# Nearest 128 keys and values moved as one 12288 B packet a partition instead of two of 6144 B

## The chip, the cores and the metric

One NeuronCore of a Trainium2 chip runs the whole kernel. The metric is the device time of one execution in microseconds. The kernel before took 404.59 us, the median of three runs (402.63, 404.59 and 405.35).

## The reference

Two decoder layers run over two groups of tokens that share the weights: a prompt of 256 tokens from position 0, and 8 sample sequences with one new token each at position 2048. Everything is float32, with a model width of 1024. Each layer normalises x, multiplies it by one input projection whose columns are split among three groups, and adds the output projection of their results to x:

```
A: a_val * sigmoid(a_glu) -> causal depthwise conv of width 31 -> LayerNorm -> silu, times silu(gate)   384 channels
B: trailing means over 2/4/8/16 positions minus the token -> 64x64 maps -> scale, times silu(gate)      256 channels
C: 6 heads of 64; keys at offsets d*j, j = 0..128, for d = 1, 4, 16; the three patterns merged by
   their softmax denominators, times silu(gate)                                                       384 channels
x = x + W_out[concat(A, B, C)]
```

For the samples the keys and values of the last 2048 positions come in as caches, one row of 384 floats (1536 B) for each sequence, position and layer. The outputs contain these caches too, moved on by one position, with the new row at the end: 8 sequences x 2047 rows x 1536 B, for keys and values and for both layers. The pattern with d = 1 needs the nearest 128 rows, the one with d = 4 every fourth row of the nearest 512, the one with d = 16 every sixteenth row of all 2048.

## The kernel before

**Who does what.** TensorE runs the projections (`pj`, 33 column tiles of 128 from `PROJ`, then 8 of the output projection, each of 8 matmuls over 264 tokens), attention and transposes. VectorE runs the 93 convolution taps of a layer (L1296), the sample scores (`tok`, `ssc`) and the products with the gates. ScalarE does the activations. The order of the steps on each engine is written out in `SCHEDULE`, `DVE_SCHEDULE` and `ACT_SCHEDULE`.

**Three DMA queues.** The queue of SP (q1 in the profile) gathers the rows that the samples attend to into `kg` and `vg` (L479, function `gather`) and stores keys back from `kg` (L459, L463, L465, function `store_rows`). The queue of ACT (q10) loads the weight tiles `wt`, 4096 B a partition and up to 14 tiles ahead (L874), and stores values back from `vg`, in the steps of the output projection (`STORES`). The queue of POOL (q0) copies the rest of the caches from HBM to HBM (L600), in packets of at most 7680 B. All three run beside each other from the start.

**The gathers.** `GATHER` cuts the 2048 rows of a sequence into three spans. The nearest one is rows 1920 to 2047, all of them: 16 partitions take 8 neighbouring rows each, which lie together in HBM and in SBUF, 8 x 1536 = 12288 B. The middle span takes every fourth row, 6 a partition, and the far span every sixteenth, 6 a partition; each of their rows is a run of 1536 B by itself. The argument `max_dma_last_dim=NEAR_BYTES` limits the run that one packet moves; with 6144 B it cuts only the runs of the nearest span, into two. There are 8 sequences, two kinds (k and v) and two layers, so 32 gathers of the nearest span, and 32 stores of it: 64 transfers of 16 partitions.

**Order on SP.** Early loads, then for layer 0 the nearest rows of `kg` (8 transfers), a table, the other spans of `kg`, all of `vg`, small loads, the stores of keys (16), a wait at L543 until these have landed, the gather of `kg` for layer 1 and so on. At the end SP stores y (L549 to L557) and then waits for every copy and store (L559 to L567).

**Waits on the gathers.** VectorE waits at L1230 for all three spans of `kg` before the first sample product (step `("sprod", 0)`, L1234). TensorE waits at L761 for `vg`. ScalarE waits at L879 for `vg` before it issues the stores of values.

Of the kernel before, what the change touches and what calls it, by code (L numbers as in the profile page):

```python
# [27 lines left out]
C_CONV, C_POOL, C_ATT, HD = 384, 256, 384, 64  # L28
# [17 lines left out]
GATHER = []  # L46
# [178 lines left out]
BLOCK_BYTES = (FAR_STEP - 1) * C_ATT * 4  # L225


NEAR_BYTES = 4 * C_ATT * 4
IN_FLIGHT = 16
assert DEPTH * NCOPIES % IN_FLIGHT == 0  # L230

# [17 lines left out]
def sample_rows(s):  # L249

    first = 2 * PER_S * (s // 2) + s % 2
    return slice(first, first + 2 * PER_S - 1, 2)
# [56 lines left out]
def trunk_program(nc, ins, const, const_at, angles, outs):  # L309
    (y_prompt, y_sample, o_conv_p, o_pool_p, o_k_p, o_v_p, o_conv_s, o_pool_s, o_k_s, o_v_s) = outs  # L310
    with ExitStack() as ctx:
# [140 lines left out]
        def store_rows(eng, kind, l, s):  # L452
# [3 lines left out]
            for (lo, d, n), name in zip(GATHER[:2], ("near", "far")):  # L456
                rows = out[:, s, lo - 1:lo - 1 + d * n * PER_S].rearrange("o (a b e) h d -> (o a) b e (h d)", a=PER_S, e=d)
                at = SLOT_OF[d]
                eng.dma_start(rows[:, :, 0, :], frm[part, at:at + n, :], max_dma_last_dim=NEAR_BYTES).then_inc(S[f"{kind}_{name}_out"], 16)  # L459
            if (kind, l) in DEEP:  # L460
# [7 lines left out]
        def _(sp):  # L468
# [3 lines left out]
            def gather(kind, l, to, name, spans=GATHER):  # L472

                for lo, d, n in spans:
                    at = SLOT_OF[d]
                    for s in SAMPLE_ORDER:
                        rows = one(f"cache_{kind}_win", l)[:, s, lo:lo + d * n * PER_S]
                        rows = rows.rearrange("o (a b e) h d -> (o a) b e (h d)", a=PER_S, e=d)[:, :, 0, :]
                        sp.dma_start(to[sample_rows(s), at:at + n, :], rows, max_dma_last_dim=NEAR_BYTES).then_inc(S[name], 16)  # L479

# [924 lines left out]
```

## Time and profile before

| | |
|---|---|
| median of the runs | 404.59 us |
| the profiled execution | 401.57 us |
| its span | 399.7 us |
| TensorE busy | 347.5 us (87%) |
| VectorE busy | 232.6 us (58%) |
| DMA | 44329 packets, 157.73 MB, mean 395 GB/s |

The span is what the profiler saw between the first and the last event; 1.9 us of the execution lie around it. DMA packets are counted one for each contiguous run that a DMA engine moves, and one for each small write to a semaphore at the end of a transfer. The core has 16 DMA engines, and a share of 100% means that all 16 moved packets all the time; since the records of neighbouring packets overlap a little, a saturated stretch shows slightly over 1.

### The profile page before, as it was taken

What the parts mean: (1) busy time and instruction counts of PE and PEld (TensorE: products, weight loads), DVE (VectorE), ACT (ScalarE), POOL (GpSimd) and SP (SyncE); (2) the same over time, 40 slices, a digit from 0 to 9 for tenths busy, and PEclk for the clock granted to TensorE, in tenths of its full rate; (3) what the DMA queues carried; (4) which work ended last, traced back from release to release, by engine and by line L of the source; (5) the groups of instructions that cost most, each with busy time, mean ns of one, the idle gap of its engine ahead of it and who ended that gap; (6) DMA issues with size and microseconds to landing.
All of it is one profiled execution on the core that took longest, in us unless ns stands there. A gap on an engine that the chain in (4) does not pass through costs nothing.

```text
span 399.7 us, 4745 instructions
## 1 busy us (share of the span) xinstructions
PE 347.5 (87%) x1550; PEld 273.4 (68%) x1550; DVE 232.6 (58%) x530; ACT 100.2 (25%) x237; POOL 58.8 (15%) x110
## 2 busy tenths in 40 slices
PE   3898799999889859899948999999979877989990
PEld 2686578887667636588827888888757654758870
DVE  2604669859977976620103489978984997541010
ACT  4200012542523123500111011453352222320011
POOL 4006830000600002044000420000600011000000
PEclk9999969999889899999986999999979988989997
DMA  8999999999999999999999999999999999999983
GB/s 293 412 419 412 418 418 417 418 407 411 417 419 408 418 392 406 396 418 418 416 398 387 414 418 416 417 411 420 418 419 417 414 357 361 372 374 372 396 347 118
DMA packets 44329, 157.73 MB, mean 395 GB/s; under 512 B 6988, under 2 KB 20116, under 8 KB 44306
## 3 DMA queue, kind: packets, MB, share of 16 engines
q0 software_dynamic: 14624, 88.25, 54.6%
q10 hardware_dynamic: 14420, 41.52, 26.3%
q1 hardware_dynamic: 15262, 27.67, 18.7%
q8 instruction: 12, 0.20, 0.2%
q14 instruction: 11, 0.09, 0.1%
HBM read 140.23 MB, written 104.46 MB: 612 GB/s over the span
## 4 chain that ended last, share of the span: by engine, by line
PE 43%; DVE 13%; SPq 12%; ACTq 11%; DMA 10%; issue 5%; ACT 4%; DVEq 0%
PE pj L693 23%; SPq L479 11%; DMA kg<-in_cache_k_win 10%; PE pj L836 8%; ACTq L459 4%; DVE yc L1296 3%; ACTq L465 3%; PE psc L765 3%; PE ptr L611 3%; DVE ssc L1240 2%; ACTq L463 2%; PE ps L813 1%; ACTq L874 1%; DVE spsum_pad L1266 1%; DVE tok L1234 1%
## 5 line engine op out<-in xcount | busy, mean ns | idle before, releaser
L693 PE MATMUL pj<-hT,wt 128*128 128x264 f32 x800 | 197.9, 407 | 6.3 <-DVE hT L1151 4.5
L693 PEld LDWEIGHTS pj<-hT,wt 128*128 128x128 f32 x800 | 159.0, 202 | 39.7 <-issue 11.6
L1296 DVE SCALAR_TENSOR_TENSOR yc<-u_ext,par,yc 128x256 f32<-128x256 f32 x180 | 77.2, 481 | 3.8 <-DVE u_smp L1180 1.0
L836 PE MATMUL pj<-mix,wt 128*128 128x264 f32 x256 | 61.2, 395 | 0.0
L836 PEld LDWEIGHTS pj<-mix,wt 128*128 128x128 f32 x256 | 49.1, 194 | 8.5
L600 POOL DMA_DIRECT2D out<-in_cache_v_win x48 | 26.2, 554 | 142.3 <-issue 142.3
L1366 DVE TENSOR_TENSOR xT<-xT,pj 128x264 f32<-128x264 f32 x16 | 6.9, 430 | 55.9 <-PE pj L836 55.9
L600 POOL DMA_DIRECT2D out<-in_cache_k_win x48 | 26.5, 561 | 83.6 <-issue 83.6
L954 ACT ACTIVATE ex<-pj 128x264 f32<-128x264 f32 x22 | 8.6, 391 | 78.3 <-PE pj L693 45.2
L1178 DVE SCALAR_TENSOR_TENSOR u_ext<-ex,pj 128x256 f32<-128x256 f32 x6 | 2.5, 422 | 30.5 <-ACT ex L954 30.5
L1234 DVE TENSOR_TENSOR tok<-kg,qb 128x1536 f32<-128x1536 f32 x10 | 17.6, 1758 | 3.4 <-DMA kg<-in_cache_k_win 3.0
L1240 DVE TENSOR_REDUCE ssc<-tok 128x24 f32<-128x1536 f32 x10 | 17.5, 1753 | 0.8 <-DVE mix L1187 0.3
L908 ACT ACT_TABLE_LOAD x12 | 15.4, 1283 | 6.7 <-issue 4.7
L765 PE MATMUL psc<-vg,spm_pad 128*64 128x384 f32 x80 | 14.9, 510 | 0.0
L1187 DVE SCALAR_TENSOR_TENSOR mix<-ex,pj 128x264 f32<-128x264 f32 x16 | 6.9, 429 | 13.3 <-ACT ex L954 12.9
L611 PE MATMUL ptr<-cst,sc 128*128 128x128 f32 x36 | 6.3, 285 | 7.0 <-DVE sc L1213 6.9
L1020 ACT ACTIVATE sc<-sc,nmax 128x128 f32<-128x128 f32 x12 | 4.8, 402 | 28.4 <-DVE nmax L1206 25.1
L1075 ACT ACTIVATE hT<-xT 128x264 f32<-128x264 f32 x8 | 3.4, 423 | 33.2 <-DVE xT L1366 26.7
L611 PEld LDWEIGHTS ptr<-cst,sc 128*128 128x128 f32 x36 | 4.0, 141 | 10.9 <-DVE sc L1213 10.5
L813 PE MATMUL ps<-yc,ones 128*128 128x264 f32 x12 | 5.2, 599 | 6.7 <-DVE yc L1296 6.7
L937 ACT ACTIVATE sqg<-pj 128x264 f32<-128x264 f32 x12 | 4.7, 391 | 24.7 <-PE pj L693 22.7
L1202 DVE SCALAR_TENSOR_TENSOR sc<-psc,cst 128x384 f32<-128x384 f32 x12 | 6.6, 553 | 6.6 <-PE psc L732 6.6
(187 smaller groups left out, 339.6 us busy)
## 6 DMA issues: line engine op xcount, KB each, us to landing
wt<-in_w_tiles ACTq DMA_DIRECT2D x62, 512.0 KB, 33.2
out<-in_cache_k_win POOLq DMA_DIRECT2D x24, 1080.0 KB, 44.4
out<-in_cache_v_win POOLq DMA_DIRECT2D x24, 1080.0 KB, 81.1
out<-in_cache_k_win POOLq DMA_DIRECT2D x8, 1200.0 KB, 72.7
out<-in_cache_v_win POOLq DMA_DIRECT2D x8, 1200.0 KB, 87.9
out<-in_cache_k_win POOLq DMA_DIRECT2D x16, 432.0 KB, 65.1
out<-in_cache_v_win POOLq DMA_DIRECT2D x16, 432.0 KB, 86.2
kg<-in_cache_k_win SPq DMA_DIRECT2D x32, 144.0 KB, 36.0
```

Source lines behind the costliest of these rows:

```text
L459: eng.dma_start(rows[:, :, 0, :], frm[part, at:at + n, :], max_dma_last_dim=NEAR_BYTES).then_inc(S[f"{kind}_{name}_out"], 16)
L465: eng.dma_start(rows[:, 0, :], frm[part.start + 2:part.stop:2, DEEP_AT, :]).then_inc(S[f"{kind}_deep_out"], 16)
L479: sp.dma_start(to[sample_rows(s), at:at + n, :], rows, max_dma_last_dim=NEAR_BYTES).then_inc(S[name], 16)
L600: pool.dma_start(dst, src, max_dma_last_dim=size).then_inc(copy_out[n % IN_FLIGHT], 16)
L611: return nc.tensor.transpose(out, in_, C["ident"][0:rows, 0:rows])
L693: last = nc.tensor.matmul(pj[n % RING][:, 0:T], wt[:, g % WRING, k, :], hT[:, k, :], start=(k == 0), stop=(k == KD - 1))
L765: nc.tensor.matmul(psc[o:o + SV_HALF, 0:C_ATT], spm_pad[:, j * NH * NS:j * NH * NS + SV_HALF], v, start=(j < 2), stop=(j >= SLOTS - 1))
L836: last = nc.tensor.matmul(pj[n % RING][:, 0:T], wt[:, g % WRING, k, :], mix[:, k, :], start=(k == 0), stop=(k == KD - 1))
L908: nc.scalar.preload_act_table_set(TABLE_BEFORE[step])
L1234: V.tensor_tensor(tok[:, :, :], kg[:, a:b, :], qb[:, None, :].to_broadcast([P, b - a, C_ATT]), ALU.mult).then_inc(S["kprod_ok"], 1)
L1240: last = V.tensor_reduce(ssc[:, a:b, :], tok[:, :, :].rearrange("p j (h d) -> p j h d", h=NH), AX.X, ALU.add)
L1296: last = V.scalar_tensor_tensor(out=yc[:, t, 0:SEQ], in0=x_w, scalar=par[:, ROW_CW + w * CT + t:ROW_CW + w * CT + t + 1], in1=yc[:, t, 0:S ...
```

## The change

`NEAR_BYTES` becomes `GATHER[0][2] * C_ATT * 4` = 8 x 384 x 4 = 12288, in place of 4 x 384 x 4 = 6144. It is used at L459 (stores of the nearest and the middle span) and L479 (gathers of all spans).

```
-NEAR_BYTES = 4 * C_ATT * 4
+NEAR_BYTES = GATHER[0][2] * C_ATT * 4
```

## Rows read from the trace of the kernel before

**Rows 1.** The page: span, engines' busy time, DMA share in 40 slices, packets
```profile
span 399.7 us, 4745 instructions
PE 347.5 (87%) x1550; PEld 273.4 (68%) x1550; DVE 232.6 (58%) x530; ACT 100.2 (25%) x237; POOL 58.8 (15%) x110
DMA  8999999999999999999999999999999999999983
DMA packets 44329, 157.73 MB, mean 395 GB/s; under 512 B 6988, under 2 KB 20116, under 8 KB 44306
```

**Rows 2.** The page's DMA queues: packets, MB, share of 16 engines over the span
```profile
q0 software_dynamic: 14624, 88.25, 54.6%
q10 hardware_dynamic: 14420, 41.52, 26.3%
q1 hardware_dynamic: 15262, 27.67, 18.7%
```

**Rows 3.** Stages: stage, length, busy time by engine, clock, DMA share, GB/s
```profile
50.00:88.00 38.00, 37.70 (x164) 31.73 (x165) 28.09 (x70) 13.37 (x33) 3.76 (x7) 0.92 1.02 414
380.00:392.00 12.00, 9.45 (x47) 7.36 (x45) 1.98 (x4) 2.22 (x5) 0.00 (x0) 1.00 0.81 314
392.00:399.70 7.70, 0.00 (x0) 0.00 (x0) 0.00 (x0) 0.00 (x0) 0.00 (x0) 0.63 0.28 101
```

**Rows 4.** Waits of SP's queue from 390 to 400 us: total, times, longest
```profile
SPq L563 <- DMA out<-vg: 5.7, 2, 4.8
SPq L561 <- DMA out<-in_cache_v_win: 0.7, 1, 0.7
```

**Rows 5.** Timeline, the last DMA that SP issues: start, duration
```profile
391.57 0.35 SPq L557 DMA_DIRECT2D out<-qk  x1
```

**Rows 6.** DMA queues from 394 to 399.7 us: packets, MB, share
```profile
q1 hardware_dynamic: 78, 0.14, 6.4%
q10 hardware_dynamic: 78, 0.12, 5.8%
```

**Rows 7.** DMA queues from 60 to 85 us: packets, MB, share
```profile
q0 software_dynamic: 924, 5.75, 55.4%
q10 hardware_dynamic: 925, 3.38, 33.3%
q1 hardware_dynamic: 927, 1.24, 13.7%
```

**Rows 8.** DMA queues from 85 to 96 us
```profile
q0 software_dynamic: 328, 1.92, 42.8%
q1 hardware_dynamic: 335, 1.34, 30.7%
```

**Rows 9.** DMA queues from 30 to 38 us: the instruction fetches
```profile
q8 instruction: 1, 0.02, 0.8%
```

**Rows 10.** Line L479, SP's gathers of keys: nanoseconds min/median/max, first and last start
```profile
L479 SPq DMA_DIRECT2D kg<-in_cache_k_win x48: 578/667/4583, 4.5 to 232.6; - x48
```

**Rows 11.** Timeline of VectorE: start, duration, instruction, idle time before it and releaser
```profile
84.83 0.56 DVE L1193 COPY qb<-ptr 128x384 f32<-128x384 f32 x1
88.35 1.76 DVE L1234 TENSOR_TENSOR tok<-kg,qb 128x1536 f32<-128x1536 f32 x1 [2.96 <-DMA kg<-in_cache_k_win]
...
270.76 0.56 DVE L1193 COPY qb<-ptr 128x384 f32<-128x384 f32 x1
```

**Rows 12.** Chain of waits in order of time, one piece in each layer
```profile
147.75 2.61 PE ps L813 x6
...
332.05 2.59 PE ps L813 x6
```

**Rows 13.** Timeline of ScalarE and its DMA queue, layer 0
```profile
46.21 0.39 ACT L954 ACTIVATE ex<-pj 128x264 f32<-128x264 f32 x1 [8.36 <-issue]
...
199.32 6.47 ACTq L459 DMA_DIRECT2D out<-vg  x2
...
205.87 3.25 ACTq L874 DMA_DIRECT2D wt<-in_w_tiles  x1
```

## The prediction

> **What bounds the kernel now.** I read the page first. TensorE is busy 87% of the span, which looks like the bound, but the DMA line shows nine tenths in every slice from the second to the 38th [rows 1]. The stages say it more sharply: from 50 to 88 us the 16 DMA engines have a share of 1.02 [rows 3]. So two things are nearly full at once, and the end of the span tells which comes last. SP issues the last store of y at 391.57 us [rows 5], and no compute engine works after 392 us [rows 3]. SP then waits 0.7 us for a cache copy and 5.7 us for stores out of vg [rows 4], that is until about 399. In the last 5.7 us the queues of SP and ACT each move 78 packets, at 6.4% + 5.8% of 16 engines, so 0.122 x 16 = 2 engines on average [rows 6]. These are engines with a backlog that the others have finished. The span has two arms, then: the compute arm, whose stores of y are issued by 391.9, and the DMA arm, which ends some 7 us later and consists of packets that an engine works off one after another since the start. I take the DMA arm as the bound. What shortens it is less packet time on the slowest engine; what only reorders packets does not.
>
> **How the three queues share an engine.** From 60 to 85 us q0, q10 and q1 moved 924, 925 and 927 packets [rows 7], though their mean sizes are 6220, 3650 and 1340 B. From 85 to 96 us, when the nearest rows of v are gathered, q0 and q1 are again equal (328 and 335) although a packet of q1 is now 4000 B [rows 8]. So an engine takes one packet of each queue in turn, whatever its size. The price of a packet follows from rows 7: share x 16 x 25 us / packets is 240 ns for q0, 144 ns for q10, 59 ns for q1. Between q0 and q1 this is 181 ns for 4885 B, 0.037 ns a byte, and 59 - 49.5 = 9.6 ns that do not depend on the size. The other two pairs of queues give 10.0 and 7.7 ns. (The whole span gives the same picture [rows 2]: 239, 117 and 78 ns for 6035, 2880 and 1813 B, 9 ns fixed.)
>
> **The change, part by part.**
>
> Packets removed. 64 transfers of 16 partitions had two packets a partition, 2048 in all; now 1024. An engine has 64 packets fewer, the bytes stay. At 9.6 ns that is 64 x 9.6 = 0.6 us off every engine, the slowest too; the bounds 7.7 and 10.0 make it 0.5 to 0.64. The Trainium skill, page "DMA: Bandwidth & Descriptors", section "Why small descriptors are slow", has a fixed cost of about 3 cycles a packet, 3.5 ns at its 850 MHz; by that the gain would be an estimated 0.2 us. The records of packets overlap a little (the share of 1.02), so the truth may lie between the two.
>
> Packets lengthened. No queue of the kernel has a packet of 12288 B: of 44329 packets 44306 are under 8 KB [rows 1]. Lower bound: the line above, 9.6 + 12288 x 0.037 = 464 ns, against 2 x 237 = 474 for the pair. Upper bound, the nearest longer packet: the one fetch of instructions from 30 to 38 us, 0.02 MB (16 KB), took 0.8% x 16 x 8 us = 1.02 us [rows 9], where the line gives 616 ns. That is 62 ns for 1000 B in place of 37 (at 16384 B), and 12288 B would cost 0.77 us, 0.29 us more than the pair. I take the line, since it holds from 1340 to 6220 B over three queues, and 12288 B lies on the same routes as 6144 B did, while the fetch ends in another place than the data.
>
> SP's queue, gathers and key stores. 32 gathers and 16 stores, in six batches of 8 transfers. In each batch an engine has 16 packets of 6144 B before and 8 of 12288 B after, so 8 turns fewer, and each turn that falls away no longer waits for one packet of q0 and one of q10: 25 us x 16 / 925 = 0.432 us a turn, of which these two take 88.7 / 102.4, 0.37 us. A batch ends 8 x 0.37 = 3.0 us earlier. Issuing itself gets no cheaper where there is room (0.58 us at least) and where there is none its length is the queue's (up to 4.58 us) [rows 10].
>
> The only wait that names a gather is VectorE's at 88.35 us, 2.96 us for kg [rows 11]. The batch of the nearest k lies ahead of those rows in the same queue, so kg lands at about 85.3 us, when qb is just ready (84.83 + 0.56 = 85.39), and the wait goes. What it is worth I read from layer 1, which does not wait there: from qb to the first ps of the convolution's norm it takes 332.05 - 270.76 = 61.29 us, in layer 0 147.75 - 84.83 = 62.92 [rows 11, 12]. So 1.6 us of compute, between 0 (if TensorE is late anyway) and 3.0.
>
> ACT's queue, value stores. There are 8 nearest stores in each layer, so an engine has 8 turns fewer for this queue. In layer 0 ScalarE is stuck in issuing at 199.32 (two stores in 6.47 us) and at 205.87 (a weight tile in 3.25 us) [rows 13], where an issue with room took 0.58 us at the least on SP [rows 10]; TensorE has nothing to do in that time. Eight turns less to drain are at most 8 x 0.43 = 3.5 us, less what the packets already drained got longer by (4 or 5 of them, 0.23 us each), 2.5 us. Against it, SP's key stores end earlier and its gather of kg for layer 1 moves forward into this stretch, up to 8 packets of 0.46 us ahead of ACT's. Net between -1 and +2.5 us; I take 1.
>
> ACT's weights early in layer 0. While the 8 long packets of the first batch pass, a turn is 0.23 us longer for ACT's queue, 8 x 0.23 = 1.8 us at worst, and once SP's queue is back to short packets 8 of these are ahead, 8 x 0.06 = 0.5 us. ScalarE is held by issuing then, 8.36 us before 46.21 [rows 13], so I count 0.5 us against compute.
>
> The sum. Compute arm: -1.6 - 1 + 0.5 = -2.1 us, and it ends near 390 instead of 391.9. It is not the last. The other gains are work in another order: an engine that serves SP's rows sooner serves the copies later, with its queues never empty. DMA arm: -0.6 us. The profiled execution of 401.57 us (span 399.7 + 1.9 around it) would become 401.0; it lies 3.0 us under the median, so for the median 404.59 - 0.6 = **404.0 us**.
>
> **The rivals.**
>
> Long packets are dear (slower). Place: every packet of 12288 B, 64 an engine. Price: by the upper bound 64 x 0.29 = 18.6 us, 423 us; halfway 414. It decides 1% from 4.05 / 64 = 63 ns over the pair, a packet of 0.54 us. For it: the only long packets in the trace are 1.6 times as dear a byte [rows 9], and they stood beside the same traffic. Against it: their destination is different, and nothing bends between 1340 and 6220 B. Chance 0.12.
>
> The compute arm sets the end after all (faster). If the late stores of vg wait for ScalarE's issue rather than for the engines' backlog, the gains pass through: 1.6 + 2.5 of the layer change and 0.6 of packets, at most 4.7 less the 0.5, so 4.2, 400.4 us. For it: ScalarE issues those stores in steps that follow TensorE. Against it: q1 and q10 have equal counts to the last [rows 6], which is what two full queues look like. Chance 0.12.
>
> The long packets hold back the others (a little slower). The Trainium skill, same page, sections "Queues, rings and completion order" and "SWDGE vs HWDGE vs iDMA", says that an engine round-robins between queues at packet granularity and that a packet should preferably be at most 4096 B. The counts of rows 7 and 8 agree with the first half. In rows of this kernel, ACT's weights are late by the 1.8 us, ScalarE keeps the delay, and y comes at 393.7: still ahead of 399, so the time stays at 404.0, and at most at 405.8 if that delay passed through. Chance 0.05.
>
> The change does nothing: packets stay cut by some limit under 8 KB, of which rows 1 (no data packet above it) say nothing either way. 404.6. Chance 0.05.
>
> **How the numbers follow.** Forecast 0.66, rivals 0.12, 0.12, 0.05, 0.05. Within 1% means 400.5 to 408.6, about what a measurement of this kernel can tell from no change. The forecast and the last two lie inside, and so does some of each of the first two: 0.78. Faster by over 1% needs nearly all of the second rival: 0.10. Slower by over 1%: the first rival, 0.12. The forecast's own range is the spread of the runs (2.0 below the median, 0.8 above) and 0 to 0.64 of gain: 402.0 to 405.4. The range goes on to the second rival's 400.4 and up to 407, a dearer packet by 40 ns, and leaves out the dear half of the first.
>
> **What would show it.** Packets down by 1024 to about 43305, with some 1024 no longer under 8 KB. The share of q1 and q10 times the span smaller by about 16 x 0.6 us in sum; if q1's share grows, long packets are dear. VectorE's wait for kg near 88 us gone. Counts of the queues still equal in a loaded stretch. The end still a wait at L563 for stores out of vg with the last DMA of SP issued some us earlier than 391.57; if instead the span shrinks with that issue, I misread the bound. It is wrong by size if 64 fixed costs are not what the slowest engine loses.

## The result, and the profile after

The changed kernel took 407.36 us, the median of 20 runs (404.56 to 408.77), against 405.13 us for the kernel before (20 runs, 402.08 to 410.0): ratio 1.0063, 95% interval 1.0045 to 1.008. In a second session beside other kernels it was 1.0088 (1.0057 to 1.0118). I had forecast a gain of 0.6 us; it is a loss of some 2.5 us. The profiled executions were 401.57 us before and 407.44 us after; the one before lies 3.6 us under its median, so their difference of 5.9 us overstates the loss.

The page of the changed kernel: span, GB/s in 40 slices, packets, and the DMA queues (packets, MB, share of 16 engines).

```profile
span 405.6 us, 4745 instructions
GB/s 281 423 412 402 416 418 409 418 383 412 419 402 409 415 383 412 417 413 410 399 362 404 414 410 413 406 371 416 418 398 419 412 343 360 377 389 380 367 372 68
DMA packets 43305, 157.73 MB, mean 389 GB/s; under 512 B 6988, under 2 KB 20116, under 8 KB 42258
q0 software_dynamic: 14624, 88.25, 54.5%
q10 hardware_dynamic: 14164, 41.52, 26.2%
q1 hardware_dynamic: 14494, 27.67, 18.6%
```

There are 1024 packets fewer and 1024 more that are not under 8 KB, so the change does what it says. But the three queues' share times the span, the time an engine spends in packets, went up where it should have gone down by 0.6 us: (54.5 + 26.2 + 18.6)% x 405.6 = 402.8 us, before 99.6% x 399.7 = 398.1 [rows 1, 2]. The GB/s line shows where. Here is that line of the kernel before:

```profile
GB/s 293 412 419 412 418 418 417 418 407 411 417 419 408 418 392 406 396 418 418 416 398 387 414 418 416 417 411 420 418 419 417 414 357 361 372 374 372 396 347 118
```

A slice is 10 us. The nearest rows of v in layer 0 pass in the 9th slice (407 before, 383 after), those of k in layer 1 in the 21st and 22nd (398, 387; after 362, 404), those of v in layer 1 in the 27th and 28th (411, 420; after 371, 416). These dips are where SP gathers nearest rows. The stretch of v in layer 1 by itself, by the DMA queues (packets, MB, share), before from 268 to 284 us:

```profile
DMA packets 1526, 6.68 MB, mean 418 GB/s; under 512 B 263, under 2 KB 385, under 8 KB 1525
q0 software_dynamic: 509, 3.14, 47.2%
q10 hardware_dynamic: 508, 1.80, 27.8%
q1 hardware_dynamic: 508, 1.73, 26.7%
```

and after, from 258 to 274 us (SP's queue is some 10 us ahead by then):

```profile
DMA packets 1313, 6.15 MB, mean 384 GB/s; under 512 B 245, under 2 KB 402, under 8 KB 1183
q0 software_dynamic: 440, 2.73, 45.1%
q1 hardware_dynamic: 434, 1.81, 29.7%
q10 hardware_dynamic: 437, 1.59, 27.2%
```

The queues still take turns one packet each. Share x 16 x length / packets is again the price of a packet. A packet of q0 cost 0.472 x 16 x 16 us / 509 = 237 ns for 6170 B before, just what my line gives, and 0.451 x 256 us / 440 = 262 ns for 6200 B after. q0 copies from HBM to HBM and has the same packets in both kernels. So the packets beside the long ones of q1 are dearer, in any queue: q10's are at 159 ns for 3640 B where the line says 144, and q1's own at 0.297 x 256 / 434 = 175 ns for 4170 B where it says 164.

Timeline of the changed kernel where VectorE starts on kg, where ScalarE starts layer 1 (its DMA queue just before), and SP's last DMA; then SP's waits at the end.

```profile
86.04 1.76 DVE L1234 TENSOR_TENSOR tok<-kg,qb 128x1536 f32<-128x1536 f32 x1 [1.02 <-DMA kg<-in_cache_k_win]
...
199.59 6.87 ACTq L459 DMA_DIRECT2D out<-vg  x2
206.54 5.65 ACTq L874 DMA_DIRECT2D wt<-in_w_tiles  x1
212.29 0.48 ACT L900 ACTIVATE r_h<-ps,cst 128x264 f32<-128x264 f32 x1 [5.36 <-issue]
...
394.02 0.35 SPq L557 DMA_DIRECT2D out<-qk  x1
```

```profile
SPq L561 <- DMA out<-in_cache_v_win: 7.9, 2, 6.3
SPq L563 <- DMA out<-vg: 2.1, 2, 1.1
```

The product that waits for kg starts 2.3 us sooner, and the wait is 1.02 us in place of 2.96 [rows 11]. The weight tile that was stuck for 3.25 us [rows 13] is stuck for 5.65, and r_h starts at 212.29 where the kernel before had

```profile
209.22 0.48 ACT L900 ACTIVATE r_h<-ps,cst 128x264 f32<-128x264 f32 x1 [2.96 <-issue]
```

The last stores of y are issued 2.4 us later than before [rows 5], and after them SP waits 10 us for copies and stores (6.4 before [rows 4]), now mostly for the cache copies of q0. The DMA arm is last in both kernels.

### The profile page after: what moved, and what is told of

It is laid out like the page before. It is cut to its first block, busy times and chain, and to the rows that moved or that the text cites. A ratio compares the mean times of both kernels' runs of the same rounds, so it can differ in the third digit from the quotient of the medians.

```text
span 405.6 us, 4745 instructions
## 1 busy us (share of the span) xinstructions
PE 341.7 (84%) x1550; PEld 268.4 (66%) x1550; DVE 232.2 (57%) x530; ACT 100.2 (25%) x237; POOL 58.6 (14%) x110
## 3 DMA queue, kind: packets, MB, share of 16 engines
q0 software_dynamic: 14624, 88.25, 54.5%
q10 hardware_dynamic: 14164, 41.52, 26.2%
q1 hardware_dynamic: 14494, 27.67, 18.6%
## 4 chain that ended last, share of the span: by engine, by line
PE 59%; DVE 13%; ACTq 11%; ACT 7%; issue 5%; DMA 2%; SPq 0%; DVEq 0%
PE pj L693 31%; PE pj L836 14%; ACTq L874 6%; DVE yc L1296 3%; PE ptr L611 3%; PE psc L765 2%; DVE ssc L1240 2%; ACTq L459 2%; DMA cst<-in_const 2%; PE ps L813 1%; ACTq L1055 1%; DVE spsum_pad L1266 1%; PE psc L611 1%; DVE sc L1202 1%; PE ps L819 1%
## 5 line engine op out<-in xcount | busy, mean ns | idle before, releaser
L693 PE MATMUL pj<-hT,wt 128*128 128x264 f32 x800 | 192.7, 399 | 8.4 <-DVE hT L1151 6.9
L693 PEld LDWEIGHTS pj<-hT,wt 128*128 128x128 f32 x800 | 154.8, 197 | 40.4 <-issue 14.0
L600 POOL DMA_DIRECT2D out<-in_cache_v_win x48 | 26.2, 553 | 146.0 <-issue 146.0
L1234 DVE TENSOR_TENSOR tok<-kg,qb 128x1536 f32<-128x1536 f32 x10 | 17.6, 1758 | 1.5 <-DMA kg<-in_cache_k_win 1.0
L765 PE MATMUL psc<-vg,spm_pad 128*64 128x384 f32 x80 | 14.6, 505 | 0.0
L1167 DVE TENSOR_TENSOR qk<-scr,r_qk 128x264 f32<-128x264 f32 x12 | 5.2, 434 | 9.6 <-ACT r_qk L902 9.4
```

The source lines that it names most:

```text
L600: pool.dma_start(dst, src, max_dma_last_dim=size).then_inc(copy_out[n % IN_FLIGHT], 16)
L693: last = nc.tensor.matmul(pj[n % RING][:, 0:T], wt[:, g % WRING, k, :], hT[:, k, :], start=(k == 0), stop=(k == KD - 1))
L765: nc.tensor.matmul(psc[o:o + SV_HALF, 0:C_ATT], spm_pad[:, j * NH * NS:j * NH * NS + SV_HALF], v, start=(j < 2), stop=(j >= SLOTS - 1))
L1234: V.tensor_tensor(tok[:, :, :], kg[:, a:b, :], qb[:, None, :].to_broadcast([P, b - a, C_ATT]), ALU.mult).then_inc(S["kprod_ok"], 1)
```

## The experiments

All are changes of the kernel before, each timed beside it. They ran in three sessions, in which the kernel before had medians of 403.17 us (gather_long, store_long, contig_short, deep_long), 399.56 us (inter_short, inter_long, half_long, contig_long) and 403.08 us (the rest). "Theory A" in the expectations is that engines meet on shared groups of partitions, "B" that a long packet is dear by itself, "C" that only the order of the work matters.

**Which side is it?** `gather_long` and `store_long` do half of the change each.

```
-  sp.dma_start(to[sample_rows(s), at:at + n, :], rows, max_dma_last_dim=NEAR_BYTES)
+  sp.dma_start(to[sample_rows(s), at:at + n, :], rows, max_dma_last_dim=2 * NEAR_BYTES)       gather_long
-  eng.dma_start(rows[:, :, 0, :], frm[part, at:at + n, :], max_dma_last_dim=NEAR_BYTES)
+  eng.dma_start(rows[:, :, 0, :], frm[part, at:at + n, :], max_dma_last_dim=2 * NEAR_BYTES)   store_long
```

> Only the gathers (L479) move 12288 B a packet; the stores stay at 6144 B. Half of the packets are saved: 32 an engine, 0.3 us. The changed kernel lost about 2.5 us. Theory A (ports): a long packet on its way into or out of SBUF waits for the other engine that uses the same group of partitions, and a wait longer than an engine can buffer holds up its next packets too; gathers run in dense batches (q1 has 4000 B a packet from 85 to 96 us), stores are spread out, so most of the loss is here: ratio 1.004 to 1.007, and q0's mean packet grows from 239 ns. Theory B (long packets dear anywhere): half of it, 1.002 to 1.004. Theory C (only the order: rows come sooner, the cache copies end later): packets keep their price, q0 239 ns and q1 78 ns plus its fewer packets; gathers advance SP's queue, ratio 1.003 to 1.006 with the last wait at L561.

> Only the stores out of kg and vg (L459) move 12288 B a packet; the gathers stay at 6144 B. Theory A: stores come spread out between shorter packets and seldom meet on a port, ratio 0.999 to 1.002. Theory B: half of the loss, 1.002 to 1.004. Theory C: the stores of values on ACT's queue are the last packets of the kernel; fewer turns for them bring them forward, ratio 0.997 to 1.001.

Measured: gather_long 1.0067 (1.0038 to 1.0096), store_long 0.998 (0.9954 to 1.0006). The gathers alone lose as much as the whole change; the stores alone lose nothing that can be measured. Their GB/s lines, gather_long first:

```profile
GB/s 288 421 405 389 415 418 411 413 415 411 415 409 408 418 377 416 416 413 408 413 369 399 414 405 418 418 352 414 421 411 399 418 370 345 380 378 378 379 375 138
```

```profile
GB/s 297 419 415 407 415 417 409 409 422 410 417 411 399 412 394 411 386 418 417 412 379 413 416 417 404 414 418 421 418 418 403 393 359 358 369 364 373 378 390 128
```

The dips of the 4th, 21st and 27th slice are in the first alone (389, 369, 352 against 407, 379, 418; the 21st is lower in both). B's equal halves did not come. Nor did C's unchanged prices: in gather_long's stretch of nearest v in layer 1, from 262 to 278 us, q0 moved 445 packets at a share of 46.1%, 265 ns each for 6180 B.

store_long also has the gain at the change of layers that I had priced at 2.5 us. Timeline of ScalarE and its queue:

```profile
199.55 3.29 ACTq L459 DMA_DIRECT2D out<-vg  x2
203.18 2.45 ACTq L874 DMA_DIRECT2D wt<-in_w_tiles  x1
205.73 0.48 ACT L900 ACTIVATE r_h<-ps,cst 128x264 f32<-128x264 f32 x1 [2.14 <-issue]
```

r_h at 205.73, 3.5 us sooner than before; in gather_long it starts at 212.94, 3.7 us later. So the two halves pull that point in opposite ways in these profiles, and in the changed kernel the gathers win.

**Do the partitions matter?** `contig_short` keeps packets of 6144 B and puts a sequence into 16 neighbouring partitions.

```
 def sample_rows(s):
-    first = 2 * PER_S * (s // 2) + s % 2
-    return slice(first, first + 2 * PER_S - 1, 2)
+    return slice(PER_S * s, PER_S * (s + 1), 1)
 ...
-                eng.dma_start(rows[:, 0, :], frm[part.start + 2:part.stop:2, DEEP_AT, :]).then_inc(S[f"{kind}_deep_out"], 16)
+                eng.dma_start(rows[:, 0, :], frm[part.start + 1:part.stop, DEEP_AT, :]).then_inc(S[f"{kind}_deep_out"], 16)
```

It leaves the masks as they are, so the samples attend to wrong rows, and only its time is of use. The partitions change for all three spans and for the stores too.

> Packets as before (6144 B), but each sequence lies in 16 neighbouring partitions (16s to 16s+15) instead of every second of 32; the masks are left as they were, so the samples' attention is computed with wrong rows. Theory A: if engines meet on groups of neighbouring partitions, 16 neighbours use half as many groups as 32, four engines on each in place of two; the packets of q1 get dearer even at 6144 B: from 85 to 96 us q1's mean packet of 4000 B goes from 161 ns to over 200, ratio over 1.01. Theories B and C: partitions do not matter, packets keep their price, ratio 0.998 to 1.002.

Measured: 1.0169 (1.0129 to 1.0208). Bytes, packets and the HBM side are those of the kernel before; only the place in SBUF differs. Its rate and packets:

```profile
GB/s 300 419 336 310 405 417 413 416 417 359 409 419 414 413 379 415 392 417 408 409 402 340 388 418 394 413 414 337 404 421 404 411 353 336 361 363 372 379 377 147
DMA packets 44329, 157.73 MB, mean 383 GB/s; under 512 B 6988, under 2 KB 20116, under 8 KB 44306
```

Dips to 310, 359, 340 and 337 in the four stretches of nearest rows, within a slice of where the changed kernel has its own, and deeper. My stretch from 85 to 96 us caught little of it, since the batch of nearest v comes mostly after it here. The batch of nearest v in layer 1 lies from 276 to 292 us:

```profile
DMA packets 1252, 5.68 MB, mean 355 GB/s; under 512 B 224, under 2 KB 263, under 8 KB 1251
q0 software_dynamic: 419, 2.58, 49.7%
q1 hardware_dynamic: 416, 1.57, 25.3%
```

A packet of q0 costs 0.497 x 256 / 419 = 304 ns for 6160 B, where the line gives 237. I had expected over 200 ns for a packet of q1 of 4000 B, and that did not come: it costs 0.253 x 256 / 416 = 156 ns for 3770 B, where the line gives 149. The loss stands mostly in the records of the other queue's packets, and I do not know why. This is the strongest single result: with the same packets, 16 neighbouring partitions in place of every second of 32 make the batches of nearest rows slower.

**Are long packets from HBM to HBM dear?** `deep_long` changes only q0.

```
-DEEP_BYTES = (DEEP_STEP - 1) * C_ATT * 4 // 3
+DEEP_BYTES = (DEEP_STEP - 1) * C_ATT * 4 // 2
```

> All rows of the nearest span stay at 6144 B; only the copies from HBM to HBM of layer 1 between the sixteenth rows go in two packets of 11520 B a block instead of three of 7680 B: 1536 packets fewer, 96 an engine, 0.9 us by the fixed cost of 9.6 ns. Theory A: no SBUF, no meeting: q0's packets cost what the line gives (9.6 + 11520 x 0.037 = 436 ns for the new ones), DMA work falls by 0.9 us, though ACT's and SP's queues wait longer in each turn. Ratio 0.996 to 1.002. Theory B: 96 pairs of long packets too dear by what the change showed (2.5 + 0.6 us for 64 packets, 48 ns each) for 192 of them: +9 us less 0.9, ratio 1.015 to 1.025. Theory C: q0 served more a turn, copies end sooner, ACT's stores later, 0.996 to 1.004.

Measured: 1.0467 (1.0442 to 1.0492), twice B's price, and neither A nor C had it. The end tells why (SP's waits, and then the GB/s line, whose last numbers are the last slices):

```profile
SPq L549 <- ACT hT L1084: 16.4, 1, 16.4
SPq L553 <- ACT hT L1087: 9.6, 1, 9.6
SPq L567 <- DMA out<-qk: 1.1, 1, 1.1
```

```profile
GB/s 294 396 405 337 387 396 368 399 410 413 420 405 397 388 407 385 391 390 385 415 411 423 368 417 414 401 412 420 406 418 419 411 413 349 366 382 376 202 172 53
```

The copies are done and SP waits for ScalarE's y. With longer packets q0 takes more of each turn, SP's and ACT's queues get fewer turns (759 from 60 to 85 us, where there were 925 [rows 7]), and the compute arm becomes the end. The rate drops to 202 and 172 GB/s there because q0 has nothing left.

So the ratio does not test B, but the packets do. Its time in packets is 97.2% x 420.0 = 408.2 us against 398.1, 10 us more, and B's price was 8. From 60 to 85 us, where SP gathers no nearest rows:

```profile
DMA packets 2283, 9.61 MB, mean 384 GB/s; under 512 B 301, under 2 KB 951, under 8 KB 1875
q0 software_dynamic: 759, 5.81, 59.0%
q10 hardware_dynamic: 763, 2.78, 29.8%
q1 hardware_dynamic: 759, 1.00, 12.1%
```

By share x 400 us / packets these are 311 ns for 7650 B in q0 (the line: 293), 156 ns for 3640 B in q10 (144), and 64 ns for 1320 B in q1 (58), at 384 GB/s in place of 416. Everything is 6 to 10% dearer, though no long packet goes into SBUF. The long packet itself follows the line: in the trace's records of single packets the 3072 of 11520 B have a median of 432 ns (the line: 436) and a mean of 451. So shared partitions are not the only way in which long packets make a stretch dearer, and what does it here stays open.

**The order of the gathers.** `inter_short` and `inter_long` gather sequence by sequence, with packets of 6144 and 12288 B; `half_short` and `half_long` keep the order of spans, and take the sequences 0, 1, 2, ... instead of 0, 4, 1, 5, ..., so that the half of the partitions no longer alternates. The two long ones have the gather line of `gather_long` as well.

```
-                for lo, d, n in spans:
-                    at = SLOT_OF[d]
-                    for s in SAMPLE_ORDER:
+                for s in SAMPLE_ORDER:
+                    for lo, d, n in spans:
+                        at = SLOT_OF[d]                                        inter_short, inter_long
-SAMPLE_ORDER = [s + PAIRS * e for s in range(PAIRS) for e in range(2)]
+SAMPLE_ORDER = list(range(NS))                                                 half_short, half_long
```

> Packets as before, 6144 B; only the order of the gathers (L474 to L479) changes: sequence by sequence (nearest, middle, far) in place of span by span; the nearest rows of k in layer 0 still go first. It is the control for inter_long. No theory has a price for it: the same packets, and the waits are for all spans together. Ratio 0.996 to 1.003.

> Gathers of 12288 B in the same order as inter_short, so that a long packet of SP's queue is followed by 12 short ones. gather_long lost 0.67%, and GB/s in its stretch of nearest v of layer 1 fell from 418 to 376. Theory A (engines meet on the same group of partitions while all gather nearest rows): the meetings are spread out, the dips in GB/s go from three of four stretches, ratio to inter_short 0.999 to 1.003. Theory B (a long packet is dear by itself): the dips only spread, the ratio stays 1.005 to 1.008 to inter_short. Theory C (order): the queues' turns saved are the same, ratio 1.004 to 1.008.

> Gathers of 12288 B; the sequences go in the order 0, 1, 2, ... 7 instead of 0, 4, 1, 5, ...: partitions 0 to 63 four times, then 64 to 127 four times, where the kernel alternates between the halves. Theory A: an engine's neighbour asks for the same group of partitions in every turn; the dips get deeper, under 376 GB/s, ratio 1.010 to 1.025. Theories B and C: the partitions don't matter, ratio as gather_long, 1.004 to 1.009.

> Control for half_long: the same order of sequences (0 to 7), packets of 6144 B. Theory A: with short packets the groups are asked for less than an engine's rate most of the time, so the order costs little: ratio 0.999 to 1.005, well under half_long's 1.011. If the order alone costs 1%, half_long says nothing on long packets.

| | ratio to before | 95% interval |
|---|---|---|
| inter_short | 0.9996 | 0.9979 to 1.0014 |
| inter_long | 1.0020 | 0.9992 to 1.0048 |
| half_short | 0.9995 | 0.9971 to 1.0020 |
| half_long | 1.0107 | 1.0082 to 1.0132 |
| gather_long (the kernel's own order) | 1.0067 | 1.0038 to 1.0096 |

The same 512 long packets cost 0.2% sequence by sequence and 1.1% with the half fixed. These two were measured in one session and their intervals are apart, so one price for all orders, as in B and C, does not fit. The kernel's own order lies between them, but its interval overlaps both. Neither order costs time with short packets. Two cautions: the medians of inter_long and inter_short, 401.37 and 399.21 us, are 0.5% apart, so inter_long may not be free; and half_short was measured in another session than half_long. In the stretch from 258 to 274 us, half_long first, then inter_long:

```profile
DMA packets 1200, 5.70 MB, mean 356 GB/s; under 512 B 235, under 2 KB 358, under 8 KB 1071
q0 software_dynamic: 404, 2.49, 45.2%
```

```profile
DMA packets 1678, 6.59 MB, mean 412 GB/s; under 512 B 230, under 2 KB 640, under 8 KB 1635
q0 software_dynamic: 559, 3.40, 52.1%
```

q0's packet is at 0.452 x 256 / 404 = 286 ns for 6160 B in half_long and 0.521 x 256 / 559 = 239 ns for 6080 B in inter_long, against 237 before and 262 in the changed kernel. In half_short, in its own stretch from 268 to 284 us, it is at 0.479 x 256 / 486 = 252 ns for 6210 B where the line gives 239, so with short packets this order has a little of the effect too. The records of single packets say the same of the gathers' own packets of 12288 B: a median of 460 ns in inter_long, 473 in gather_long and 506 in half_long, where the line gives 464.

**Both at once.** `contig_long` is contig_short with gathers of 12288 B.

> Gathers of 12288 B into 16 neighbouring partitions a sequence (wrong rows for the samples' attention, as in contig_short, which cost 1.7% at 6144 B). Theory A: four engines on a group, each with up to half of its time in such a packet: over 1.035, more than the sum of the two (1.017 and 1.007). Theory B: the sum, 1.022 to 1.027. Theory C: the same as B.

Measured: 1.0417 (1.0364 to 1.0469), above A's bound and far above B's sum. Two cautions. As in deep_long, the span ends with the stores of y and no wait for a copy or a store of rows, so the compute arm is the end here and the 4.2% is not packet time alone. And its six runs spread from 413.12 to 425.21 us. Its packets of 12288 B have a median of 556 ns.

**The fixed cost of a packet.** `near_3072` goes the other way, for gathers and stores.

```
-NEAR_BYTES = 4 * C_ATT * 4
+NEAR_BYTES = 2 * C_ATT * 4
```

> Nearest rows in four packets of 3072 B: 2048 packets more, 128 an engine. The step of my sum: 9.6 ns a packet, 1.2 us, ratio 1.003. If only 4 to 5 ns of a packet are real engine time (records overlap), 0.6 us, 1.0015. Theory A adds nothing (no long packet), or takes something away if 6144 B packets already meet.

Measured: 1.0423 (1.0383 to 1.0462), fourteen times what I expected, so the fixed cost is not what it shows. Timeline of VectorE and SP:

```profile
94.59 1.76 DVE L1234 TENSOR_TENSOR tok<-kg,qb 128x1536 f32<-128x1536 f32 x1 [10.99 <-DMA kg<-in_cache_k_win]
...
414.58 0.35 SPq L557 DMA_DIRECT2D out<-qk  x1
```

With 16 turns more in the first batch kg comes at 94.59 instead of 88.35, 6.2 us later; my 0.37 us a turn gives 16 x 0.37 = 5.9. SP's queue is late in every batch, TensorE waits for vg as well, and y is issued 23 us later. The rule of the turns was right, and it has a cliff on this side: the compute arm becomes the bound. The time in packets, 97.4% x 417.3 = 406.5 us, is larger too, by more than 128 fixed costs; where that is from I did not trace.

**A better version.** `inter_store` takes the two halves that cost nothing: gathers of 6144 B in the order of inter_short, stores of 12288 B. `after_again` is the changed kernel beside it.

> The candidate: gathers of 6144 B sequence by sequence (inter_short, 0.9996), stores of 12288 B (store_long, 0.998). Theory A: both are free of the meetings, 32 packets an engine are saved, 0.15 to 0.3 us: ratio 0.996 to 1.001.

> The changed kernel once more, for its ratio beside the other three and a second profile: 1.004 to 1.009, with a dip in GB/s in the slices of the nearest k and v of layer 1.

Measured: inter_store 0.9962 (0.994 to 0.9983), 401.57 us against 403.08, and after_again 1.0088 (1.0057 to 1.0118), 406.83 us. inter_store is ahead of both, of the kernel before by 0.4%. Its y is issued by 386.8 and SP then waits 9.2 us for copies at L561, so the DMA arm bounds it. In after_again the time in packets is 99.1% x 406.2 = 402.5 us, as in the first profile (402.8).

## Why the prediction was wrong

**Two arms, the DMA arm last: right.** In before, after, gather_long, half_long and inter_store the span ends with waits for copies and stores, after y has been issued. Where the compute arm comes last (deep_long, contig_long, near_3072) the time in packets falls to 97.2 to 97.9% of the span.

**One packet of each queue in turn: right.** Counts are equal in every stretch shown, and near_3072 confirmed the 0.37 us a turn (6.2 us measured, 5.9 worked out). kg came 2.3 us sooner where I said 3.0, and 1.02 us of the wait that was to go were left.

**"I take the line, since it holds from 1340 to 6220 B": the step that failed.** The term was 64 packets at 464 ns in place of 128 at 237. What failed is the assumption that a packet's price depends on its size alone. The long packet holds to the line in a calm stretch (a median of 460 ns in inter_long and for the stores, against 464), so the bend that I weighed as a rival is not there: my upper bound of 18.6 us was far too high. What the term left out is what happens in a stretch where all engines gather nearest rows: everything in it gets dearer, 237 to 262 ns for a packet of q0. The size of the term, from the time in packets: 402.8 and 402.5 us in the two profiles of the changed kernel, against 398.1, 397.3 and 401.1 in three with gathers and stores of 6144 B (before, inter_short, half_short), whose mean is 398.8. That is 3.8 us more where I had -0.6, and the three differ by as much among themselves; the ratios say 2.5 to 3.5. The other profiles fall on the same two sides: 402.4 and 403.0 us with long gathers in dense batches (gather_long, half_long), 400.8, 398.8 and 398.5 in store_long, inter_store and inter_long. The rival of the dear long packet had the sign but not the place: I bound it to every long packet, and the stores' cost nothing that could be measured, while deep_long's came to more than its price.

**What makes them dear.** Shown: the cost sits in the gathers; it depends on which partitions neighbouring engines write (contig_short, at unchanged packet size); and it depends on the order of the gathers (half_long against inter_long, in one session), where the packets and their partitions are the same and only what stands beside what differs. Argued from that: engines that write into the same small group of partitions share its rate. A sequence's 16 rows lie in every second of 32 partitions. If a group is a few neighbouring partitions, two engines share one here and four in contig_short. By the prices of rows 7 and the line, a packet of q1 is 237 of a turn's 621 ns at 6144 B (with q0's 240 and q10's 144 ns), but 464 of 848 at 12288 B. So two engines ask a group for an estimated 0.76 of an engine's rate before and 1.09 after, and in contig_short four ask for 1.53. If a group takes one engine's rate, which no run shows, it is enough in the first case and not in the others. The estimate leaves out q10's weights, which go to all partitions.

The Trainium skill, page "SBUF — State Buffer", section "Door 1: The DMA port swizzle", says that four neighbouring partitions, and those 32 further on, share a port, that the port changes with the upper 64, and that DMA bandwidth depends on how many ports are reached. contig_short and half_long agree with it, with the 1.7% and 1.1% above. My prediction did not ask where in SBUF a packet lands.

Two things stay open. In contig_short the loss stands in q0's packets (304 ns) and hardly in q1's own (156), which the shared rate by itself does not explain. And deep_long made all packets 6 to 10% dearer with long packets that never touch SBUF, so a second cause, of which a part may be in the changed kernel too, is not excluded.

**The change of layers: right in its parts, wrong in the net.** I took 1 us of gain from -1 to +2.5. The stores alone gave 3.5 us (store_long), but the earlier gather of kg for layer 1, which I did name, took 6.6 of it back in the changed kernel: r_h is 3.1 us later than before. Its price was too low. It counted 8 packets at 0.46 us and not what they do to the others; that this is the difference is argued, and inter_long supports it, where the gather is as early (200.28 us) and r_h starts at 209.72, as in inter_short (209.66).

**Packets removed, 0.6 us: open.** No run isolates it. With 32 packets fewer an engine, worth 0.3 us, store_long gained 0.8 us, which its interval doesn't tell from nothing, and inter_store 1.5 us, so something else is in there (perhaps that the stores of v get through sooner).

## What to carry to other kernels

A price per packet that fits a line over the sizes in a trace need not hold for a stretch full of longer ones, even where the longer packet by itself stays on the line. Ask how many engines write into the same group of partitions at that moment, and for what part of their turns. Where several queues share the DMA engines in turns of one packet, packet size is a share: making one queue's packets longer or shorter moves every other queue. In this kernel, with compute and DMA nearly level, both ways cost over 4% (deep_long, near_3072). Test gathers and stores apart: here one half lost 0.7% and the other, with a change of order, gained 0.4%.

## What I had not expected of the hardware

A packet from HBM to HBM gets dearer by a tenth (237 to 262 ns for the same bytes, and 286 in half_long) beside another queue's packets into SBUF on the same engines; in contig_short it costs 304 ns beside packets of unchanged size. And splitting the nearest rows into 3072 B, 2048 packets more of 44329, cost 4.2%, where 128 fixed costs an engine would be 0.3%: y was issued 23 us later, and VectorE and TensorE waited for SP's rows (L1234 for kg 20.0 us in all in place of 3.0, L765 for vg 6.5 us, where the kernel before has no such wait).
